# Rotated q and k computed by feature instead of by token in a two-block transformer kernel on one core

## The chip, the core and the metric

One core of a Trainium2 chip runs the whole program in one launch. The metric is device time in microseconds (us) of that launch. Four compute engines run their own instruction streams in order and meet on semaphores: TensorE (PE: matmuls and transposes, out to PSUM), VectorE (DVE), ScalarE (ACT) and GpSimd (POOL). SyncE (SP) issues the loads of the weights.

## The reference, cut to what matters

A block with two kinds of attention and a feed-forward part is followed by a second block of two layers over 256 tokens of 1024 features. The change is in the second block:

```python
def rope(x, pos):                       # MLA (64 of 192 features of a head), MoBA (64)
    cos, sin = jnp.cos(ang), jnp.sin(ang)
    x1, x2 = x[..., : d // 2], x[..., d // 2:]
    return jnp.concatenate([x1 * cos - x2 * sin, x1 * sin + x2 * cos], -1)

def retnet_rotate(x, pos):              # retention: 256 features, partners are neighbours
    x1, x2 = x[..., 0::2], x[..., 1::2]
    out = jnp.stack([x1 * cos - x2 * sin, x2 * cos + x1 * sin], -1)

# even layer: retention of 4 heads of 256 and MLA of 8 heads side by side, one output projection
q_r, k_r = retnet_rotate(_heads(rq, 4), pos), retnet_rotate(_heads(rk, 4), pos)
q_pe, k_pe = rope(q_m[..., 128:], pos), rope(mkr[:, None], pos)
# odd layer: MoBA of 16 heads of 64; with 256 tokens it is causal attention
q, k = rope(_heads(q, 16), pos), rope(_heads(k, 16), pos)
```

Every feature of a rotated head is its own value times a cosine plus its partner's value times a sine.

## The kernel before, in words

All weights come as 235 pieces of 128 x 1024 numbers. Each is split by ScalarE (`w_hi`, L1061) and VectorE (`w_lo`, L1205) into two parts, and TensorE forms every product as three matmuls (L792 to L794). A *chunk* is the set of pieces of one projection; a ring of six split pieces lies ahead of TensorE. A chunk of kind A (4 pieces, 512 output features) has the tokens as its output rows: 48 matmuls that stream 512 weight columns. A chunk of kind F (1 or 2 pieces, 128 features each) has the features as its output rows: 24 matmuls a piece that stream 256 tokens. Kind C is `mqkv`, the latents of MLA, by token.

`plan()` writes one list of steps, ORDER, and each engine runs its own part of it in that order. Jobs (a pair of attention heads: `scores`, `soft` on VectorE, `exp` on ScalarE, `norm` on VectorE, `pt` and `pv` on TensorE) wait in `pending` and are put, one step after each half piece, between the matmuls of later chunks, as soon as the names they need are in `given`. When a chunk's last matmul has been listed, its `evac` step follows at once.

Rotated chunks (`rk`, `rq` of retention, `mk`, `mq` of MoBA, 512 features each, and the 256 features of `mlaq`) are by token. VectorE multiplies with cosine (L1238) and sine (L1240, L1241), GpSimd adds and subtracts (L1538, L1539), and TensorE turns the result (`turn` steps on `rot`, L977), 2 x 2 transposes at a time; ScalarE copies them to `qT`, `kT` or `qpeT` (L1066). The turns are listed no earlier than four half pieces after the `evac` (`TURN_WAIT`), and only then is the chunk's name given. `kpe`, the rotated part of MLA's k, is 64 columns of `mqkv` with a turn of its own. The angle tables (L1375 to L1388 on VectorE, L1185 and L1186 on ScalarE) are made between the last up projection and the down projection of the first block; the split of the next pieces stands behind them on both engines.

Of the kernel before, what the change touches and what calls it, by code (L numbers as in the profile page):

```python
# [18 lines left out]
ALU = mybir.AluOpType  # L19
# [42 lines left out]
def chunks():  # L62
# [28 lines left out]
    for j in range(FT):  # L91
# [6 lines left out]
    add("mqkv", "C", 8, "X", k8, "dve", ("rms",),  # L98
        ("w_in_even", None, cols(MQ, 256) + cols(MKR, 32) + cols(MKV, 256) + cols(MKR + 32, 32)))

    def mla(half):
        for a in (0, 1):
# [5 lines left out]
             + [c for h in heads for c in cols(192 * h + 128, 64)]), after_job=16 + 4 * half)  # L108
# [4 lines left out]
    def ret_qk(pair):  # L113
        for name, c0 in (("k", RK), ("q", RQ)):
            add(f"r{name}{pair}", "A", 4, "X", k8, "dve", ("rope", name, 1 - pair, 256),
                ("w_in_even", None, [c0 + 256 * h + c for h in (2 * pair, 2 * pair + 1) for c in even_perm]),
                after_job=24 * pair)
# [9 lines left out]
    ret_qk(0)  # L127
    mla(1)
    for r in (0, 1):
        ret_vg(r)  # L130
    ret_qk(1)
# [5 lines left out]
    for half in (0, 1):  # L137
        s = 1 - half
# [3 lines left out]
        add(f"mv{half}", "A", 4, "X", k8, "act", ("copy_tok", s), ("w_in_odd", None, cols(2048 + 512 * half, 512)),  # L142
            after_ret=4)
        for a in (0, 1):
            add(f"mgt{half}{a}", "F", 2, "X", k8, "dve", ("gate", s, a),
                ("w_in_odd", None, cols(3072 + 512 * half + 256 * a, 256)), after_ret=4)
# [42 lines left out]
for h in range(8):  # L189
    JOBS.append(dict(kind="mla", s=0, h=h % 4, qk=[f"mlaq{h // 4}", f"mlakv{h // 4}"], v=f"mlakv{h // 4}",  # L190
                     g=f"mg{h // 4}{h // 2 % 2}", tile=h))
for h in range(16):
    JOBS.append(dict(kind="moba", s=1 - h // 8, h=h % 8, qk=[f"mk{h // 8}", f"mq{h // 8}"], v=f"mv{h // 8}",
                     g=f"mgt{h // 8}{h // 4 % 2}", tile=h // 2))
# [14 lines left out]
def plan():  # L209

    order, given, pending, deferred = [], set(), [], []
    state = dict(hi=0, lo=0, wait=0, credit=0)
# [31 lines left out]
    def flush_turns():  # L244

        while deferred:
            rope_turns()

    def evacuate(c):
        name, kind = CH[c]["name"], CH[c]["evac"][0]  # L250
        if kind in ("rope", "mla_q", "rms"):
            flush_turns()
        emit(("evac", c))
        if kind in ("rope", "mla_q"):
            deferred.append((name, 0))
            state["wait"] = TURN_WAIT
        else:
            given.add(name)

    def run(name, rate, needs=lambda i: set(), early=0, between=(), tail=()):  # L260
# [13 lines left out]
        for x, half in enumerate(halves):  # L274
# [24 lines left out]
            if deferred:  # L299
                state["wait"] -= 1  # L300
                if state["wait"] <= 0:
                    rope_turns()
# [8 lines left out]

    def rope_turns():

        name, i = deferred.pop()
        kind = CH[BY[name]]["evac"]
        dst = ("attn", kind[1], kind[2]) if kind[0] == "rope" else ("qpe",)
        emit(("turn", new_t(("rot", i), dst + (i,), False, 3, BY[name], 2)))
        if kind[0] == "rope" and i == 0:
            deferred.append((name, 2))
        else:  # L320
            given.add(name)
# [37 lines left out]
    def retention(r):  # L359
        s = set([f"rk{r // 2}", f"rq{r // 2}"])  # L360
# [57 lines left out]
    for name in ("mg00", "mg01"):  # L418
# [7 lines left out]
    for name in ("rk0", "rq0"):  # L426
        run(name, 1)
# [13 lines left out]
    for name in ("rk1", "rq1"):  # L441
        run(name, 1)
# [12 lines left out]
    rest = norm_second(2, CH[BY["mk0"]]["u0"] + 3)  # L455
# [47 lines left out]
for _s in ORDER:  # L503
    if _s[0] == "turn":
# [6 lines left out]
        else:  # L511
            _seen[d[:3] if d[0] == "attn" else d[:1]] = ("turn", _s[1])
# [3 lines left out]
    elif _s[0] in ("mm", "scores", "ret_s"):  # L516
        FILLED[_s] = dict(_seen)

ROT_READ, _r = {}, None
for _s in ORDER:  # L520
    if _s[0] == "turn" and TJ[_s[1]]["src"][0] in ("rot", "mn", "kpe"):
        _r = _s[1]
    elif _s[0] == "evac":
        ROT_READ[_s[1]] = _r
# [5 lines left out]
for _name, _n in (("ident", P), ("causal", 3 * P), ("band", P), ("cumA", 4), ("cumB", 4),  # L530
                  ("inv64", 32), ("inv256", 128)):
# [5 lines left out]
def constants():  # L537
# [17 lines left out]
    put("inv64", (1.0 / (np.float32(10000.0) ** (np.arange(0, 64, 2, dtype=np.float32) / np.float32(64)))).astype(np.float32)[None, :])  # L555
# [1082 lines left out]
```

## Time and profile before

| | us |
|---|---|
| median of 3 runs | 821.38 (820.64 to 822.02) |
| the profiled execution | 821.49 |
| its span, first to last instruction | 819.7 |
| TensorE busy | 767.2 (94%) |
| VectorE busy | 517.0 (63%) |
| ScalarE busy | 390.9 (48%) |
| GpSimd busy | 78.4 (10%) |

Times in the rows are counted from the span's start. The ends of matmuls are modelled, so the cost of one is read from start to start. A number in brackets at a row's end is the idle time of its engine before it, and what ended it. The granted clock is a share of TensorE's 2.4 GHz; 0.50 is 1.2 GHz.

### The profile page before, as it was taken

Reading aid. Unit: us, or ns where it says so; the run is one execution under the profiler, and the core shown is the slowest. Engines: PE = TensorE matmul, PEld = TensorE weight load, DVE = VectorE, ACT = ScalarE, POOL = GpSimd, SP = SyncE. Lnnn points to the kernel's source line nnn. Section 1 sums busy time; section 2 is a strip of 40 time slices with the busy share of each in tenths; the row PEclk is TensorE's granted clock in tenths of the full one; section 3 lists DMA queues with packets and bytes.
Section 4 is the critical chain, followed back from the end, with each engine's and each line's share of the span. In section 5 each row is a group of like instructions: output and inputs, shape, how many; then the busy total and the mean of one; then the engine's idle time right before and its main releaser. Section 6 shows DMA issues by size and latency. Waiting matters only on the chain.

```text
span 819.7 us, 12104 instructions
## 1 busy us (share of the span) xinstructions
PE 767.2 (94%) x4530; PEld 651.9 (80%) x4530; DVE 517.0 (63%) x910; ACT 390.9 (48%) x645; POOL 78.4 (10%) x98
## 2 busy tenths in 40 slices
PE   6999997999999999798988999999999989999995
PEld 5986875999999878697778777777788867777774
DVE  4554667677777764774565465855574497567575
ACT  5554662665656453264445544343434333563650
POOL 0000000011111100011031000220000014004000
PEclk9999999899999999999999999999999999999999
DMA  9742343455656574165326336344666616435402
GB/s 332 282 154 79 112 138 138 154 190 171 203 165 197 170 279 141 55 217 181 105 93 196 110 103 205 123 143 147 205 225 190 200 52 210 151 114 168 156 27 78
DMA packets 37291, 130.28 MB, mean 159 GB/s; under 512 B 4401, under 2 KB 4657, under 8 KB 37105
## 3 DMA queue, kind: packets, MB, share of 16 engines
q1 hardware_dynamic: 36000, 125.04, 46.0%
q0 software_dynamic: 1232, 4.46, 1.7%
q8 instruction: 37, 0.61, 0.3%
q14 instruction: 22, 0.17, 0.1%
HBM read 128.43 MB, written 1.05 MB: 158 GB/s over the span
## 4 chain that ended last, share of the span: by engine, by line
PE 83%; DVE 9%; POOL 3%; ACT 2%; issue 2%; DMA 1%; DVEq 0%; SPq 0%; ACTq 0%
PE acc L792 25%; PE acc L794 23%; PE acc L793 23%; PE acc L903 2%; PE acc L977 2%; PE acc L922 1%; POOL rot L1538 1%; PE acc L942 1%; POOL rot L1539 1%; DVE small L1401 1%; DVE res L1425 1%; DVE res L1393 1%; PE acc L901 1%; DVE res L1435 1%; DMA res<-in_x 1%
## 5 line engine op out<-in xcount | busy, mean ns | idle before, releaser
L1205 DVE TENSOR_TENSOR w_lo<-raw,w_hi 128x1024 fp32r<-128x1024 f32 (+2 forms) x235 | 282.6, 1228 | 89.5 <-ACT w_hi L1061 89.4
L1061 ACT ACTIVATE w_hi<-raw 128x1024 fp32r<-128x1024 f32 (+2 forms) x235 | 237.5, 1036 | 73.6 <-PE acc L794 66.3
L792 PE MATMUL acc<-X_hi,w_hi 128*128 128x256 f32 x616 | 179.0, 291 | 3.9 <-DVE w_lo L1205 2.9
L793 PE MATMUL acc<-X_lo,w_hi 128*128 128x256 f32 x616 | 176.3, 286 | 0.0
L794 PE MATMUL acc<-X_hi,w_lo 128*128 128x256 f32 x616 | 176.1, 286 | 0.0
L792 PE MATMUL acc<-w_hi,X_hi 128*128 128x512 f32 (+1 forms) x352 | 141.7, 402 | 9.3 <-DVE X_lo L1212 4.5
L794 PE MATMUL acc<-w_hi,X_lo 128*128 128x512 f32 (+1 forms) x352 | 135.4, 385 | 0.0
L793 PE MATMUL acc<-w_lo,X_hi 128*128 128x512 f32 (+1 forms) x352 | 135.2, 384 | 0.0
L792 PEld LDWEIGHTS acc<-X_hi,w_hi 128*128 128x128 f32 x616 | 120.2, 195 | 8.5 <-issue 4.0
L793 PEld LDWEIGHTS acc<-X_lo,w_hi 128*128 128x128 f32 x616 | 120.4, 195 | 0.1
L794 PEld LDWEIGHTS acc<-X_hi,w_lo 128*128 128x128 f32 x616 | 120.2, 195 | 0.0
L792 PE MATMUL acc<-w_hi,S_hi 128*128 128x512 f32 (+1 forms) x264 | 104.2, 395 | 2.4 <-DVE w_lo L1205 2.4
L793 PE MATMUL acc<-w_lo,S_hi 128*128 128x512 f32 (+1 forms) x264 | 102.1, 387 | 0.0
L794 PE MATMUL acc<-w_hi,S_lo 128*128 128x512 f32 (+1 forms) x264 | 102.0, 386 | 0.0
L792 PEld LDWEIGHTS acc<-w_hi,X_hi 128*128 128x128 f32 x352 | 66.8, 190 | 26.6 <-issue 10.1
L794 PEld LDWEIGHTS acc<-w_hi,X_lo 128*128 128x128 f32 x352 | 66.8, 190 | 13.1
L793 PEld LDWEIGHTS acc<-w_lo,X_hi 128*128 128x128 f32 x352 | 67.0, 190 | 11.4 <-issue 0.7
L792 PEld LDWEIGHTS acc<-w_hi,S_hi 128*128 128x128 f32 x264 | 49.6, 188 | 14.3 <-DVE w_lo L1205 2.8
L1306 DVE SCALAR_TENSOR_TENSOR v<-acc,cvp,v 128x255 f32<-128x255 f32 (+1 forms) x88 | 38.4, 478 | 32.6 <-ACT v L1126 31.8
L794 PEld LDWEIGHTS acc<-w_hi,S_lo 128*128 128x128 f32 x264 | 49.6, 188 | 10.3
L793 PEld LDWEIGHTS acc<-w_lo,S_hi 128*128 128x128 f32 x264 | 49.7, 188 | 9.5 <-issue 0.2
L1126 ACT ACTIVATE v<-acc,cvp 128x256 f32<-128x256 f32 x44 | 22.5, 562 | 50.4 <-PE acc L794 50.4
(147 smaller groups left out, 729.2 us busy)
## 6 DMA issues: line engine op xcount, KB each, us to landing
raw<-in_w SPq DMA_DIRECT2D x225, 512.0 KB, 4.2
raw<-in_w SPq DMA_DIRECT2D x8, 288.0 KB, 2.8
gate<-in_ln_gain POOLq DMA_DIRECT2D x4, 512.0 KB, 4.3
gate<-in_ln_bias POOLq DMA_DIRECT2D x4, 512.0 KB, 4.9
res<-in_x SPq DMA_DIRECT2D x4, 256.0 KB, 3.6
gate<-in_bias SPq DMA_DIRECT2D x1, 1024.0 KB, 10.3
out<-res SPq DMA_DIRECT2D x4, 256.0 KB, 2.1
decay<-in_decay SPq DMA_DIRECT2D x1, 512.0 KB, 10.3
```

Source lines behind the costliest of these rows:

```text
L792: nc.tensor.matmul(out, a_hi, b_hi, start=start, stop=False)
L793: nc.tensor.matmul(out, a_hi, b_lo, start=False, stop=False)
L794: return nc.tensor.matmul(out, a_lo, b_hi, start=False, stop=stop)
L901: nc.tensor.matmul(dst, qT[s][:, h, q], kT[s][:, h, 0:nk], start=True, stop=False)
L903: last[i] = nc.tensor.matmul(dst, qT[s][rows, h // 2, q], kT[s][rows, h // 2, 0:nk], start=True, stop=kind != "fox")
L922: last = nc.tensor.transpose(job[:, 2, b * P:(b + 1) * P], pr[:, j % 2, b * P:(b + 1) * P], ident)
L942: last = nc.tensor.matmul(job[i * HD:(i + 1) * HD, 3, q0:q0 + n], vv[s][:, tt, v], ptb[:, (j + i) % 2, b0:b0 + n], start=tt == 0, stop=tt ...
L977: last = nc.tensor.transpose(out[:, i * S + tt * P:i * S + (tt + 1) * P], src[:, i * P:(i + 1) * P], ident)
L1061: nc.scalar.activation(w_hi[:, u % RING, 0:n], raw[:, u % RAW, 0:n], ACT.Copy).then_inc(hi_done, 1)
L1126: last = nc.scalar.activation(conv[j % 2][:, i, :], acc[:, b0, i * S:(i + 1) * S], ACT.Identity, scale=cvp[:, 2, i, j:j + 1], bias=cvp[:, ...
L1205: nc.vector.tensor_tensor(w_lo[:, u % RING, 0:n], raw[:, u % RAW, 0:n], w_hi[:, u % RING, 0:n].bitcast(F32), ALU.subtract).then_inc(lo_don ...
L1306: last = nc.vector.scalar_tensor_tensor(o, acc[:, b0, i * S:i * S + S - lag], cvp[:, 2 - lag, i, j:j + 1], o, ALU.mult, ALU.add)
```

## The change

Rotated chunks become kind F: their features are the output rows, as `qT` and `kT` want them, and nothing rotated is transposed. A retention head is a chunk of its own (`rk0` to `rk3`, `rq0` to `rq3`); MoBA's `mk` and `mq` are four chunks of 256 features each; the rotated columns of `mlaq` are by feature too, and `kpe` is a chunk of one piece, its 64 columns twice. `mqkv` keeps 2 x 256 columns a token instead of 2 x 288.

Of a head of 256, the partners lie in the two 128-row tiles. Of a head of 64, weight columns are permuted (`turn_perm`) so that partners are 16 rows apart in a group of 32; VectorE's shuffle exchanges them. The tables have one row a feature and one column a token (128 x 256, for 64 and for 256), from positions that are loaded to all 128 partitions. GpSimd multiplies by the sine, then adds, each over 128 x 512 (for 256: as before, two of 128 x 256). Attention waits for `rope_done`, which GpSimd's last step sets. A name is given with its `evac` step. In MoBA the order of the chunks is new, and all 16 heads are listed as one sequence.

```diff
+    turn_perm = [32 * e + 16 * g + i for g in (0, 1) for e in (0, 1) for i in range(16)]
-        ("w_in_even", None, cols(MQ, 256) + cols(MKR, 32) + cols(MKV, 256) + cols(MKR + 32, 32)))
+    add("mqkv", "C", 8, "X", k8, "dve", ("rms",), ("w_in_even", None, cols(MQ, 256) + cols(MKV, 256)))
+    add("kpe", "F", 1, "X", k8, "dve", ("rope", "kpe", 0, 0, 64), ("w_in_even", None, [MKR + i for i in turn_perm] * 2))
...
-            add(f"r{name}{pair}", "A", 4, "X", k8, "dve", ("rope", name, 1 - pair, 256),
+            add(f"r{name}{r}", "F", 2, "X", k8, "dve", ("rope", name, 1 - r // 2, 2 * (r % 2), 256),
...
-            add(f"m{name}{half}", "A", 4, "X", k8, "dve", ("rope", name, s, 64), ("w_in_odd", None, cols(c0 + 512 * half, 512)),
-                after_ret=4, by_token=(name, half) == ("k", 0))
+            add(f"m{name}{half}{a}", "F", 2, "X", k8, "dve", ("rope", name, 1 - half, 2 * a, 64),
+                ("w_in_odd", None, [c0 + 512 * half + 256 * a + 64 * h + i for h in range(4) for i in turn_perm]), after_ret=4)
...
     def evacuate(c):
-        name, kind = CH[c]["name"], CH[c]["evac"][0]
-        if kind in ("rope", "mla_q", "rms"):
-            flush_turns()
         emit(("evac", c))
-        if kind in ("rope", "mla_q"):
-            deferred.append((name, 0))
-            state["wait"] = TURN_WAIT
-        else:
-            given.add(name)
+        given.add(CH[c]["name"])
...
-    emit(("turn", new_t(("kpe", 0), ("kpe", 0), False, 3, 0)))
     for i in (0, 2):
-        emit(("turn", new_t(("mn", i), ("S", 20 + i), True, 3, 0, 2)))
+        emit(("turn", new_t(("mn", i), ("S", 20 + i), True, i // 2, 0, 2)))
...
-    run("mk0", 0, early=3, between=rest)
-    run("mq0", 0)
-    attention(range(24, 32))
-    for name in ("mv0", "mgt00", "mgt01", "mk1", "mq1"):
-        run(name, 1)
-    attention(range(32, 40))
-    for name in ("mv1", "mgt10", "mgt11"):
+    run("mv0", 0, early=3, between=rest)
+    for name in ("mk00", "mq00", "mgt00"):
+        run(name, 0)
+    attention(range(24, 40))
+    for name in ("mk01", "mq01", "mgt01", "mk10", "mq10", "mv1", "mgt10", "mk11", "mq11", "mgt11"):
         run(name, 1)
...
-        ang = qT[0][:, 0:2, 0:160]
+        ang = qT[0][:, 0:2, :]
...
+                    if BY[name] in ROPES:
+                        pe.wait_ge(rope_done, ROPES.index(BY[name]) + 1)
...
+                cos = tab[:, 0, int(wide), :].unsqueeze(1).to_broadcast([P, nt, S])
+                if wide:
+                    sin = tab[:, 1, 1, :]
+                    nc.vector.tensor_tensor(part[:, 0, :], x[:, 1, :], sin, ALU.mult)
+                    nc.vector.tensor_tensor(part[:, 1, :], x[:, 0, :], sin, ALU.mult)
+                else:
+                    nc.vector.stream_shuffle(part, x, [i ^ 16 for i in range(32)])
+                nc.vector.tensor_tensor(out, x, cos, ALU.mult).then_inc(evac_dve, 1)
...
+                if rope_width(c) == 256:
+                    nc.gpsimd.tensor_tensor(out[:, 0, :], out[:, 0, :], part[:, 0, :], ALU.subtract)
+                    nc.gpsimd.tensor_tensor(out[:, 1, :], out[:, 1, :], part[:, 1, :], ALU.add).then_inc(rope_done, 1)
+                else:
+                    nc.gpsimd.tensor_tensor(part, part, sin, ALU.mult).then_inc(pool_chain, 1)
+                    pool.wait_ge(pool_chain, chained[0])
+                    nc.gpsimd.tensor_tensor(out, out, part, ALU.add).then_inc(rope_done, 1)
```

Three places show how the steps move. The first is TensorE where the first scores of MoBA's second half of heads stand (`pr` transposes are L905 and L922, scores L886 and L903). Before, behind the first half of the third piece of `mv1`, with the second turn of `mq1` between:

```order
L793 MATMUL acc<-w_lo,X_hi 128x512
L794 MATMUL acc<-w_hi,X_lo 128x512
L977 MATMUL acc<-cst,rot 128x128 [waits rot_ready,t_hi]
L977 MATMUL acc<-cst,rot 128x128
L977 MATMUL acc<-cst,rot 128x128 [waits rot_ready]
L977 MATMUL acc<-cst,rot 128x128
L903 MATMUL acc<-kT,qT 128x128 [waits t_hi,max_done]
```

Now, behind the last matmuls of `mq10`:

```order
L774 MATMUL acc<-X_lo,w_hi 128x256
L775 MATMUL acc<-X_hi,w_lo 128x256
L905 MATMUL acc<-cst,pr 128x128 [waits pt_copied,p_done]
L905 MATMUL acc<-cst,pr 128x128 x2
L886 MATMUL acc<-kT,qT 128x128 [waits rope_done,max_done]
```

Between the last matmul of the rotated q and the scores that read it, five half pieces of `mv1` and two turns have become three transposes of `pr`; the scores wait for GpSimd itself. The scores of heads 12 to 15 stand behind `mq11` in the same way, those of heads 4 to 7 one half piece behind `mq01`, and those of heads 0 to 3 five half pieces behind `mq00`.

The second place is VectorE for the same chunk (L1205 and L1194 are splits of weights, L1333 and L1313 the softmax of the scores above). Before:

```order
L1238 TENSOR_TENSOR rot<-acc,tab 128x512 [waits t_ready,rot_ready,ry_done,w_used]
L1240 TENSOR_TENSOR rtmp<-acc,tab 128x8x32
L1241 TENSOR_TENSOR rtmp<-acc,tab 128x8x32
L1238 TENSOR_TENSOR rot<-acc,tab 128x512
L1240 TENSOR_TENSOR rtmp<-acc,tab 128x8x32
L1241 TENSOR_TENSOR rtmp<-acc,tab 128x8x32
L1205 TENSOR_TENSOR w_lo<-raw,w_hi 128x1024 [waits w_used,hi_done] x2
L1333 ISA pr,small<-acc,cst 128x128 [waits pt_ready,sc_ready]
```

Now:

```order
L1194 TENSOR_TENSOR w_lo<-raw,w_hi 128x1024 [waits w_used,hi_done] x2
L1223 STREAM_SHUFFLE rtmp<-acc 128x512 [waits rope_done,ry_done,w_used]
L1224 TENSOR_TENSOR qT<-acc,tab 128x512
L1313 ISA pr,small<-acc,cst 128x128 [waits pt_ready,sc_ready]
L1313 ISA small 128x1
```

Six instructions for 512 features are two for 256, and the softmax follows with no split between. The third place is VectorE behind `mq01` (L1321 to L1323 are the `norm` of head 3, for which the `pt` after the next half piece waits). Now:

```order
L1194 TENSOR_TENSOR w_lo<-raw,w_hi 128x1024 [waits w_used,hi_done]
L1223 STREAM_SHUFFLE rtmp<-acc 128x512 [waits rope_done,ry_done,w_used]
L1224 TENSOR_TENSOR qT<-acc,tab 128x512
L1321 RECIPROCAL small<-small 128x2 [waits exp_done]
L1322 TENSOR_SCALAR pr<-pr,small 128x128 [waits dve_chain]
L1323 TENSOR_SCALAR pr<-pr,small 128x256
```

A rotation stands ahead of a `norm` there; it does so behind `mk01`, `rk0` and `rq0` too. Before, no rotation of MoBA stood ahead of a `norm`.

## Rows read from the trace of the kernel before

**Rows 1.** the page's part 4, the chain that ended last: shares by engine
```profile
PE 83%; DVE 9%; POOL 3%; ACT 2%; issue 2%; DMA 1%; DVEq 0%; SPq 0%; ACTq 0%
```

**Rows 2.** TensorE by stretch: length, busy (instructions), granted clock, DMA
```profile
153.00:273.00 120.00, 120.00 (x1002) 1.00 0.56 184
606.68:640.68 34.00, 34.00 (x151) 1.00 0.67 218
352.60:358.20 5.60, 5.60 (x45) 1.00 0.98 328
```

**Rows 3.** TensorE's timeline: start, duration, work, [idle before <- its releaser]
```profile
684.07 0.38 PE L977 MATMUL acc<-cst,rot 128*128 128x128 f32 x2
...
685.28 0.48 PE L792 MATMUL acc<-w_hi,X_hi 128*128 128x512 f32 x1
...
686.76 0.60 PE L977 MATMUL acc<-cst,rot 128*128 128x128 f32 x4
687.11 0.48 PE L792 MATMUL acc<-w_hi,X_hi 128*128 128x512 f32 x1
```

**Rows 4.** TensorE's waits in 359:660, then in 676:800: us in total, times, longest
```profile
PE acc L792 <- ACT kT L1088: 3.2, 2, 1.6
PE acc L922 <- DVE pr L1343: 2.1, 1, 2.1
...
PE acc L977 <- POOL rot L1539: 1.3, 2, 0.6
...
PE acc L977 <- POOL rot L1539: 1.9, 3, 0.6
PE acc L922 <- DVE pr L1343: 1.7, 4, 0.4
PE acc L903 <- ACT qT L1066: 1.6, 2, 0.8
```

**Rows 5.** timeline of TensorE around the transposes of the latents
```profile
371.58 0.38 PE L977 MATMUL acc<-cst,ryb 128*128 128x128 f32 x2
...
375.18 0.36 PE L792 MATMUL acc<-S_hi,w_hi 128*128 128x256 f32 x1
```

**Rows 6.** the largest wait, and two stretches with their granted clock
```profile
142.85 1.09 PE L961 MATMUL acc<-cst,res 128*128 128x128 f32 x4 [4.69 <-DVE res L1435]
...
143.00:150.35 7.35, 6.93 (x31) 0.50 0.17 50
375.60:379.05 3.45, 3.45 (x19) 0.51 0.00 0
```

**Rows 7.** timelines of TensorE, VectorE and GpSimd around rotations
```profile
691.31 0.39 PE L792 MATMUL acc<-w_hi,X_hi 128*128 128x512 f32 x1
...
691.51 0.69 DVE L1238 TENSOR_TENSOR rot<-acc,tab 128x512 f32<-128x512 f32 x1 [1.31 <-PE acc L794]
...
410.65 0.81 DVE L1343 TENSOR_SCALAR pr<-pr,small 128x256 f32<-128x256 f32 x1
...
382.16 0.47 POOL L1538 TENSOR_TENSOR rot<-rot,rtmp 128x128 f32<-128x128 f32 x1 [18.86 <-DVE rtmp L1241]
...
692.94 0.74 POOL L1538 TENSOR_TENSOR rot<-rot,rtmp 128x256 f32<-128x256 f32 x1 [7.91 <-DVE rtmp L1241]
...
694.34 1.72 POOL L1538 TENSOR_TENSOR rot<-rot,rtmp 128x256 f32<-128x256 f32 x1
```

**Rows 8.** timelines of VectorE, ScalarE, TensorE around the angle tables
```profile
279.52 0.27 DVE L1375 CAST small<-posi 128x2 f32<-128x2 int32 x1
...
281.15 1.54 DVE L1383 SCALAR_TENSOR_TENSOR qT<-qT 128x320 f32<-128x320 f32 x3
...
284.57 0.26 ACT L1185 ACTIVATE tab<-kT 128x64 f32<-128x64 f32 x1 [4.13 <-DVE kT L1388]
...
287.84 0.50 PE L792 MATMUL acc<-w_hi,S_hi 128*128 128x512 f32 x1 [2.39 <-DVE w_lo L1205]
```

**Rows 9.** timeline of ScalarE: the copy of v of the first MLA half
```profile
388.72 1.03 ACT L1091 ACTIVATE v<-acc 128x1024 f32<-128x1024 f32 x1
```

More of the change, by code:

```diff
@@ L107, in mla @@
             ("w_uq_even", [0, 1], [c for h in heads for c in cols(192 * h, 128)]
-             + [c for h in heads for c in cols(192 * h + 128, 64)]), after_job=16 + 4 * half)
+             + [192 * h + 128 + i for h in heads for i in turn_perm]), after_job=16 + 4 * half)
         add(f"mlakv{half}", "Q2", 2, "S", [22, 23], "act", ("mla_kv", half),
@@ L127, in chunks @@
     ret_qk(0)
+    ret_qk(1)
     mla(1)
@@ L310, in run @@
                 state["credit"] -= 1
[L312 to L321, printed above, removed]
     def attention(jobs):
@@ L425, in plan @@
     attention(range(16, 20))
-    for name in ("rk0", "rq0"):
+    for name in ("rk0", "rq0", "rk1", "rq1"):
         run(name, 1)
@@ L440, in plan @@
         run(name, 1)
-    for name in ("rk1", "rq1"):
+    for name in ("rk2", "rq2", "rk3", "rq3"):
         run(name, 1)
@@ L511 @@
         else:
-            _seen[d[:3] if d[0] == "attn" else d[:1]] = ("turn", _s[1])
+            raise ValueError(d)
     elif _s[0] == "ylo":
@@ L515 @@
             _seen[("S", JOBS[_j]["tile"])] = ("y", _s[1] // 2)
-    elif _s[0] in ("mm", "scores", "ret_s"):
+    elif _s[0] == "mm":
         FILLED[_s] = dict(_seen)
[L519 to L524, printed above, removed]
+MN_TURN = [_s[1] for _s in ORDER if _s[0] == "turn" and TJ[_s[1]]["src"][0] == "mn"]
 RET_TURN = {r: max((n for n in RANK if TJ[n]["src"][:2] == ("ry", r)), key=RANK.get) for r in range(4)}
@@ L618, in build @@
         rgain = pr[:, :, :].rearrange("p b n -> p (b n)")[:, 0:512]
[L619 to L624 removed]
+        ang = qT[0][:, 0:2, :]
+        turns = qT[0][:, 2:4, :]
+        wrap = qT[1][:, 0:2, :]
+        sin_arg = kT[0][:, 0:2, :]
+        cos_arg = kT[0][:, 2:4, :]
+        posi = ptb[:, 0, 0:S].bitcast(I32)
+        posf = ptb[:, 1, 0:S]
+        latent = rot
         bforget = small[:, 80:81]
@@ L870, in mm @@
                                          hi[:, k, :], lo[:, k, :], x == 0, x == 1)
+                elif kind == "Q1":
+                    for x, k in enumerate(tiles):
+                        w = slice(x * 256 + part * P, x * 256 + part * P + P)
+                        last = three(acc[:, b0 + 2, part * S:(part + 1) * S], wh[:, w], wl[:, w], hi[:, k, :], lo[:, k, :],
+                                     x == 0, x == 1)
                 else:
-                    n = 256 if kind == "Q1" else 512
                     for x, k in enumerate(tiles):
-                        w = slice(x * n, x * n + n)
-                        last = three(acc[:, b0 + 2 + part, 0:n], hi[:, k, part * P:(part + 1) * P],
+                        w = slice(x * 512, x * 512 + 512)
+                        last = three(acc[:, b0 + 2 + part, :], hi[:, k, part * P:(part + 1) * P],
                                      lo[:, k, part * P:(part + 1) * P], wh[:, w], wl[:, w], x == 0, x == 1)
@@ L889, in scores @@
                 bank_free(pe, step)
-                seen = FILLED[step]
-                if kind in ("mla", "moba"):
-                    keys = [("qpe",), ("kpe",)] if kind == "mla" else [("attn", "q", s), ("attn", "k", s)]
-                    pe.wait_ge(t_hi, max(RANK[seen[k][1]] for k in keys) + 1)
                 for tt, c0, nk in ((0, 0, P), (1, P, S)):
@@ L1032, in y_dest, with rope_dest, rope_width, rope_part @@
             return S_hi[:, tile, :], S_lo[:, tile, :], yb[:, j // 2 % 2 * S:(j // 2 % 2 + 1) * S]
+        def rope_dest(c):
+            e = CH[c]["evac"]
+            if e[0] == "mla_q":
+                return qpeT[:, :, :]
+            if e[1] == "kpe":
+                return kpeT[:, :, :]
+            return (qT if e[1] == "q" else kT)[e[2]][:, e[3]:e[3] + 2, :]
+        def rope_width(c):
+            return 64 if CH[c]["evac"][0] == "mla_q" else CH[c]["evac"][4]
+        def rope_part(c):
+            nt = rope_dest(c).shape[1]
+            return rtmp[:, ROPES.index(c) % 2, 0:nt * S].rearrange("p (k s) -> p k s", k=nt)
         def t_dest(n):
@@ L1215, in rope @@
                 ch = CH[c]
-                kind = ch["evac"][0]
-                heads, d = (512 // ch["evac"][3], ch["evac"][3]) if kind == "rope" else (1, 64) if kind == "rms" else (4, 64)
-                b0, half, r = ch["bank"], d // 2, ROT.index(c)
-                tab = tab64 if d == 64 else tab256
+                r, out, part = ROPES.index(c), rope_dest(c), rope_part(c)
+                nt = out.shape[1]
+                bank = ch["bank"] + (2 if ch["evac"][0] == "mla_q" else 0)
+                x = acc[:, bank, 0:nt * S].rearrange("p (k s) -> p k s", k=nt)
```

192 lines of the change are left out of this document (70 added, 122 removed).

## The prediction, made before the changed kernel ran

> **What bounds the kernel now.** I read the chain that ended last first: TensorE holds 83% of it [rows 1]. So time changes by what TensorE has to do and by what it waits for, and nothing else. The second view gives its price of work, from start to start. In a stretch of F chunks 1,000 matmuls of 256 columns (two more hang over the edges) take 120 us: 0.120 each. In a stretch of 512-column matmuls 150 take 34.0 us: 0.2267 each. In `mqkv` 42 of 288 columns take 5.60 us: 0.133 each [rows 2]. The third view is the turns. One that waits for nothing takes 0.35 (686.76 to 687.11), one that waits 0.64 for GpSimd takes 1.21 (684.07 to 685.28), so such a wait costs 0.2 more than its own length; and the first matmul behind a turn lasts 0.48 where others last 0.39, 0.1 more [rows 3]. The fourth is TensorE's waits: in both layers of the second block they belong mostly to this change's parts [rows 4]. The fifth is the clock: behind a wait of 4.69 it was half for 7.35 us of TensorE's work, and it was half once more right behind the turns of the latents; waits of 2.1 and 2.39 left it up [rows 4, 6, 8].
>
> **What goes.** 18 turns of rotated tiles (8 chunks of two, `mlaq` two) at 0.35 and about 0.1 behind each: 8.0. Their waits: for GpSimd 1.3 + 1.9, for the copy of q 1.6 and once more in retention, which I take as 0.8, and 3.2 where the copy of `kT` stood on ScalarE behind the copy of a turn [rows 4]: 8.8, and 0.2 more for each of ten: 2.0. From the turn of `kpe` to the first `mlaq` matmul 3.60 go by [rows 5]. The two turns of the latents now use two banks and need not wait for each other; what is left is one turn, ScalarE's copy and VectorE's difference, two operations of 128x512 at 0.7 [rows 7] and 0.3 to drain, with hops 2.2: 1.4 saved. With less idle time there the stretch at half clock, 3.45 us long, should go: half of it, 1.6 [rows 6]. Sum: **-21.8**.
>
> **What TensorE must do more.** Eight A chunks of 48 x 0.2267 = 10.88 become 96 x 0.120 = 11.52: +5.1. `mqkv` falls by 96 x 0.0133 = 1.3, `kpe` adds 24 x 0.120 = 2.9: +1.6. Sum: **+6.7**.
>
> **The angle tables.** VectorE works from 279.52 to 284.5 on them, ScalarE ends them, and only then comes the split for which TensorE waits 2.39 [rows 8]. They grow from 320 to 512 numbers a row. At nothing but a fixed cost they would add 0, in full proportion 0.6 x 5.0 = 3.0. One such operation over 320 takes 0.51 (281.15), one over 512 about 0.69 (691.51) [rows 7, 8], 35 to 40% more: +2.0 with ScalarE's part. This path has no cover, so the wait becomes 4.4. That lies near the 4.69 that cost the clock. Half clock costs half its length, between 0 and 3.7 (7.35 / 2) [rows 6], 1.7 for a stretch like the one at 375; with the chance that it comes I take 1.5. Sum: **+3.5**.
>
> **The rotation as a wait.** VectorE starts 0.20 after TensorE's next start (691.31, 691.51), and 128x512 from PSUM takes it 0.69 [rows 7]. The shuffle has no row. Its bounds are half of that and double; I take the same 0.69, since it streams as many numbers. The Trainium skill, "VectorE: DVE Perf Modes", section on the perf-mode tier table, gives about 2400 ns for a shuffle of 2048 numbers with no faster mode; an estimate from that page is 0.6 for 512. GpSimd takes 0.47 for 128x128 and 0.74 for 128x256 [rows 7], 0.27 per 128, so 1.28 for 512; bounds are 0.74 and the 1.72 of an operation that was held up. GpSimd's two depend on each other. The Trainium skill, "GPSIMD Engine Reference", section "Elementwise — side-by-side cycle accounting", has 2.6 cycles a number for two inputs; an estimate is 1.1 for 512 without the start, and that page speaks against arithmetic on this engine. Chain: 0.20 + 2 x 0.69 + 0.1 + 1.28 + 0.1 + 1.28 = 4.35 us from the chunk's end to the scores.
>
> What covers it decides. In retention 10 us of other chunks do, and before MoBA's first scores five half pieces (7.2 us); no wait there, even if each GpSimd operation is held 1 us by a split. Before the scores of heads 8 and of 12 there is only one `pt` (three transposes, like a turn 0.35): 4.0 each, **+8.0**. TensorE's whole queue stands behind them; VectorE's next is the softmax of the same scores. Each such wait may cost the clock, 1.4 each by chance: **+2.8**. Behind `mv1` follows its first `pv` directly: 0.2 + 1.03 for the copy [rows 9] + 0.1: **+1.3**.
>
> Then the `norm` behind a rotation. At 410.65 an operation of VectorE over 128x256 took 0.81 beside GpSimd's rotation, more than the 0.69 of one twice as wide [rows 7]; so behind a rotation `norm` first waits for one GpSimd operation. `mk01`: 0.20 + 1.38 + 0.1 + 1.28 + 0.3 = 3.3 against `pt` and a half piece, 1.8: **+1.5**. `mq01`: the scores of heads 4 to 7 need both GpSimd operations and, between them, the `norm`: 4.5 against 2.2 (`pt`, half piece, `pt`): **+2.3**. `rk0` and `rq0` have 128x256 operations: 1.3 each, for which the 2.1 there now goes: about 0. Of the four waits of 0.43 for `pr` two go: **-0.9**.
>
> **Sum:** -21.8 + 6.7 + 3.5 + 8.0 + 2.8 + 1.3 + 1.5 + 2.3 - 0.9 = +3.4. The profiled execution took 821.49, so 824.9; it stands 0.1 above the median. I say **825**. The 18 copies that ScalarE loses and the load of positions on SyncE's queue I cost at nothing: ScalarE runs ahead of TensorE there, and the load has five raw pieces ahead of it; without that cover it would be a microsecond or two once.
>
> **Rivals.** *The clock stays up.* The three long waits come, but none halves it, as 2.39 did not: 825 - 4.3 = 820.7. For it: only one wait of this length is in the trace, and at 4.69 it is longer than all of mine. Against: at 375 less sufficed. 0.20.
>
> *Faster: GpSimd's operation hardly grows.* If 128x512 costs the 0.74 of 128x256, the chain is 2.2 of GpSimd's time less 1.1, that is 1.1 shorter: 3.3 at three scores, 0.5 at `mk01`, and the two long waits of 2.9 then leave the clock up, 2.8: 825 - 6.6 = 818.4. It decides below some 0.85 an operation. Against it: 0.47 to 0.74. 0.13.
>
> *Slower still: GpSimd holds back the splits.* An operation of GpSimd beside a split of two SBUF inputs took 1.72 for 0.74: they take turns [rows 7]. Now one of GpSimd's lasts 1.28 and there are 16 in MoBA. Where four of them end in a late `w_lo`, that is 4 x 1.28 = 5.1: 830. It decides where VectorE falls behind its lead of four pieces; the place is `mk01` and `mq01`, where each chunk's splits, rotation, two softmaxes and two norms stand beside 2.6 us of GpSimd. For it speaks that every rotation in the trace was held up so, against it that TensorE waited for no `w_lo` behind one. The Trainium skill, "SBUF — State Buffer", section "Who interferes with whom", calls this port pair an exclusive lock that the loser waits out; the trace agrees with 1.72 for 0.74. 0.22.
>
> **Numbers.** My forecast holds 0.45: 822 to 828. A measurement tells about 0.2%, 1.6 us, from no change: faster is below 819.8, slower above 823.0. Forecast: 0.40 slower, 0.05 same. Clock stays up: 0.05 faster, 0.13 same, 0.02 slower. Small GpSimd cost: 0.13 faster. Port: 0.22 slower. Faster 0.18, same 0.18, slower 0.64. Of the bounds, a shuffle of half or double time moves three scores by 1.0 to 2.1, the tables move it by -2.0 to +1.0. Leaving a tenth at each end: 818.5 to 830.5.
>
> **What would show it.** No matmul on `rot`; F matmuls at 0.120; the wait at the first down pieces 4.4 instead of 2.39, the shuffle at 0.7; a wait of 4 for GpSimd before two `scores`, of 1 before one more, and 1.3 before one `pv`; the clock at half behind some of them; no waits for `kT` of 1.6. It is wrong if the waits before the scores are under 3 us, if the removed waits come back elsewhere in the even layer (the `pt` behind `rk0`, the first MLA scores behind `mlakv`), or if `w_lo` ends waits in MoBA.

## The result and the profile after

| | before | after |
|---|---|---|
| median | 821.15 us (820.64 to 822.02, 4 runs) | 827.65 us (4 runs; the three that count: 825.02, 826.69, 828.62) |
| ratio after / before | | 1.0072, 95% interval 1.0049 to 1.0096 |
| the profiled execution | 821.49 | 828.62 |
| its span | 819.7 | 826.8 |
| TensorE's mean granted clock | 0.987 | 0.978 |

The change makes the kernel 0.7% slower. The fourth run of after took 1087 us at a mean clock of 0.654; it is in the median and not in the ratio, and differences from the changed kernel are taken below from 826.69, the middle one of the three that count. The profiled execution is the slowest of those three: what is read from it adds up to 7.1 us, where the medians (826.69 and 821.15) lie 5.5 apart. The kernel before, measured beside every experiment, took 821.04 to 821.54. The page of the changed kernel, first the busy times, then the shares of the chain that ended last, answers to [rows 1]:

```profile
PE 768.2 (93%) x4864; PEld 670.5 (81%) x4864; DVE 524.3 (63%) x901; ACT 382.1 (46%) x625; POOL 89.8 (11%) x88
...
PE 84%; DVE 9%; issue 2%; ACT 2%; DMA 1%; POOL 1%; SPq 0%; DVEq 0%; ACTq 0%
```

TensorE is busy 1.0 us longer than before and the span is 7.1 longer: what was added is waiting. (A matmul at half clock counts as busy for longer, so some of the 1.0 is clock as well.) The totals of TensorE's waits, the even layer first (359:660), then MoBA (670:805), answer to [rows 4]:

```profile
PE acc L905 <- DVE pr L1323: 2.7, 2, 1.3
PE acc L773 <- DVE gate L1240: 1.5, 1, 1.5
...
PE acc L886 <- POOL qT L1509: 9.7, 3, 4.9
PE acc L905 <- DVE pr L1323: 3.1, 3, 1.3
PE acc L925 <- ACT v L1076: 1.1, 1, 1.1
```

In the even layer (retention and MLA) the waits for `kT`, for `rot` and for `qT` are gone. In MoBA three `scores` (L886) wait for GpSimd for 9.7 us in all. Next I cut both executions at five places where TensorE starts the same piece of work; each number is the difference of two start times, and the five sum to the spans:

| TensorE from ... to ... | before | after | difference | by the terms of the prediction |
|---|---|---|---|---|
| start to the first up projection | 145.45 | 146.58 | +1.1 | none: nothing there is touched |
| to the down matmul behind the tables | 142.39 | 144.41 | +2.0 | +2.0 |
| to the first matmul of `mqkv` | 52.03 | 53.58 | +1.6 | +1.5 |
| to the first matmul of MoBA | 324.10 | 313.53 | -10.6 | -9.5 |
| to the end of MoBA's layer and of the program | 155.73 | 168.70 | +13.0 | +9.5 |

The first row is a start that differs from execution to execution: over all profiles of this study the `turn` ahead of it begins anywhere from 141.9 to 144.0. The last column splits the terms by layer: the even one loses ten turns (4.4), waits (5.3 and 1.0), 1.4 at the latents and 1.6 of clock, and gains 1.6 and 2.6 of work; MoBA loses eight turns (3.6), waits (3.5 and 1.0) and 0.9, and gains 2.6 of work and 8.0 + 2.8 + 1.3 + 1.5 + 2.3.

**The tables.** ScalarE, VectorE and TensorE, as [rows 8] before:

```profile
287.40 0.63 ACT L1173 ACTIVATE tab<-kT 128x512 f32<-128x512 f32 x1 [5.71 <-DVE kT L1367]
...
288.64 4.83 ACT L1051 ACTIVATE w_hi<-raw 128x1024 fp32r<-128x1024 f32 x5
289.71 5.76 DVE L1194 TENSOR_TENSOR w_lo<-raw,w_hi 128x1024 fp32r<-128x1024 f32 x5 [2.35 <-ACT w_hi L1051]
290.99 0.50 PE L773 MATMUL acc<-w_hi,S_hi 128*128 128x512 f32 x1 [4.29 <-DVE w_lo L1194]
```

The wait is 4.29 where 2.39 was. All three engines take part in it: VectorE computes the angles, ScalarE takes the sines and then splits, and VectorE idles 2.35 for that split.

**The scores of head 8.** VectorE, GpSimd and TensorE behind `mq10`; its last matmul ends just before 734.32:

```profile
733.23 2.36 DVE L1194 TENSOR_TENSOR w_lo<-raw,w_hi 128x1024 fp32r<-128x1024 f32 x2 [1.43 <-ACT w_hi L1051]
734.32 0.49 PE L905 MATMUL acc<-cst,pr 128*128 128x128 f32 x3
...
735.52 0.73 DVE L1223 STREAM_SHUFFLE rtmp<-acc 128x512 f32<-128x512 f32 x1
736.14 0.67 DVE L1224 TENSOR_TENSOR qT<-acc,tab 128x512 f32<-128x512 f32 x1
736.89 1.26 POOL L1507 TENSOR_TENSOR rtmp<-rtmp,tab 128x512 f32<-128x512 f32 x1 [4.27 <-DVE qT L1224]
738.23 1.26 POOL L1509 TENSOR_TENSOR qT<-qT,rtmp 128x512 f32<-128x512 f32 x1
739.75 1.65 PE L886 MATMUL acc<-kT,qT 64*128 64x128 f32 x8 [4.94 <-POOL qT L1509]
```

The chain of the prediction stands there link by link: shuffle, multiply, two GpSimd operations of 1.26. From the shuffle's start it takes 4.23. The shuffle itself starts 1.2 after the chunk's end, 1.0 later than it could: two splits stand ahead of it. Behind `mq11` nothing does; there TensorE waits 3.95, and from the chunk's end (776.93) to the scores (781.37) 4.44 go by, for which I had 4.35.

**The norm behind a rotation.** VectorE, GpSimd and TensorE behind `mk01`:

```profile
697.67 0.67 DVE L1224 TENSOR_TENSOR kT<-acc,tab 128x512 f32<-128x512 f32 x1
...
698.42 1.26 POOL L1507 TENSOR_TENSOR rtmp<-rtmp,tab 128x512 f32<-128x512 f32 x1 [8.11 <-DVE kT L1224]
698.45 1.32 DVE L1322 TENSOR_SCALAR pr<-pr,small 128x128 f32<-128x128 f32 x1
699.69 0.34 DVE L1323 TENSOR_SCALAR pr<-pr,small 128x256 f32<-128x256 f32 x1
...
700.09 0.55 PE L905 MATMUL acc<-cst,pr 128*128 128x128 f32 x3 [1.35 <-DVE pr L1323]
```

The same L1322 takes 0.28 where GpSimd rests (715.72); here it takes 1.32 and ends with GpSimd's operation.

**The clock.** TensorE by stretch, with the granted clock behind the counts:

```profile
291.68:295.09 3.41, 3.41 (x10) 0.50 0.93 299
...
711.52:714.93 3.41, 3.41 (x17) 0.50 0.02 5
738.82:745.65 6.83, 5.90 (x18) 0.50 0.12 43
779.78:786.61 6.83, 5.24 (x25) 0.50 0.25 79
```

These four are at half clock; the kernel before had none behind its tables and none in MoBA. It had two in the even layer, the one at 375.60 [rows 6] and one at 348.33, the first of the rows here. In this execution they are gone; the second row is the changed kernel from behind the tables into MoBA, at full clock throughout:

```profile
348.33:351.74 3.41, 3.41 (x16) 0.50 0.50 150
...
296.00:700.00 404.00, 387.28 (x2226) 1.00 0.50 164
```

Half of TensorE's time in a stretch at half clock is the loss. In MoBA these are 3.41 / 2 + 5.90 / 2 + 5.24 / 2 = 7.3, in the even layer -3.4.

The second 1.7 of that -3.4 is not the change's doing. The stretch at 348.33 begins among the short waits at the start of `mqkv`, which stand in every kernel here, and nine of the twelve profiled executions are at half clock there (this row is from the changed kernel with its tables moved, see below):

```profile
344.77:348.18 3.41, 3.31 (x15) 0.50 0.36 96
```

The three that are not are the changed kernel, the kernel before with its tables moved, and `norm_first`. That the clock stayed up there in the changed kernel's profile is chance, as far as these runs show.

### The profile page after: what moved, and what is told of

The parts are those of the page before. It is cut to its first block, busy times and chain, and to the rows that moved or that the text cites. A ratio compares the mean times of both kernels' runs of the same rounds, so it can differ in the third digit from the quotient of the medians.

```text
span 826.8 us, 12730 instructions
## 1 busy us (share of the span) xinstructions
PE 768.2 (93%) x4864; PEld 670.5 (81%) x4864; DVE 524.3 (63%) x901; ACT 382.1 (46%) x625; POOL 89.8 (11%) x88
## 4 chain that ended last, share of the span: by engine, by line
PE 84%; DVE 9%; issue 2%; ACT 2%; DMA 1%; POOL 1%; SPq 0%; DVEq 0%; ACTq 0%
PE acc L773 25%; PE acc L775 24%; PE acc L774 24%; PE acc L886 2%; PE acc L925 1%; DVE small L1380 1%; DVE res L1404 1%; PE acc L905 1%; DVE res L1372 1%; PE acc L884 1%; DMA res<-in_x 1%; DMA raw<-in_w 1%; DVE res L1414 1%; ACT w_hi L1051 1%; DVE X_lo L1201 1%
## 5 line engine op out<-in xcount | busy, mean ns | idle before, releaser
L1194 DVE TENSOR_TENSOR w_lo<-raw,w_hi 128x1024 fp32r<-128x1024 f32 (+1 forms) x236 | 285.4, 1236 | 91.1 <-ACT w_hi L1051 91.0
L1051 ACT ACTIVATE w_hi<-raw 128x1024 fp32r<-128x1024 f32 (+1 forms) x236 | 237.7, 1034 | 87.2 <-PE acc L775 80.8
L773 PE MATMUL acc<-X_hi,w_hi 128*128 128x256 f32 x880 | 256.4, 291 | 3.9 <-DVE w_lo L1194 2.9
L774 PE MATMUL acc<-X_lo,w_hi 128*128 128x256 f32 x880 | 252.2, 287 | 0.0
L775 PE MATMUL acc<-X_hi,w_lo 128*128 128x256 f32 x880 | 251.9, 286 | 0.0
L773 PEld LDWEIGHTS acc<-X_hi,w_hi 128*128 128x128 f32 x880 | 172.2, 196 | 10.6 <-issue 6.0
L773 PE MATMUL acc<-w_hi,S_hi 128*128 128x512 f32 x256 | 102.5, 400 | 4.3 <-DVE w_lo L1194 4.3
L775 PE MATMUL acc<-w_hi,S_lo 128*128 128x512 f32 x256 | 100.4, 392 | 0.0
L774 PE MATMUL acc<-w_lo,S_hi 128*128 128x512 f32 x256 | 100.3, 392 | 0.0
L773 PE MATMUL acc<-w_hi,X_hi 128*128 128x512 f32 (+1 forms) x224 | 88.8, 396 | 6.2 <-DVE X_lo L1201 4.5
```

Source lines behind the costliest of these rows:

```text
L773: nc.tensor.matmul(out, a_hi, b_hi, start=start, stop=False)
L774: nc.tensor.matmul(out, a_hi, b_lo, start=False, stop=False)
L775: return nc.tensor.matmul(out, a_lo, b_hi, start=False, stop=stop)
L1051: nc.scalar.activation(w_hi[:, u % RING, 0:n], raw[:, u % RAW, 0:n], ACT.Copy).then_inc(hi_done, 1)
L1194: nc.vector.tensor_tensor(w_lo[:, u % RING, 0:n], raw[:, u % RAW, 0:n], w_hi[:, u % RING, 0:n].bitcast(F32), ALU.subtract).then_inc(lo_don ...
```

## The experiments

My theory after the result was that the change itself saves time, and that it is slower because of where its results are waited for: two `scores` right behind their rotated q, a `norm` behind the rotation, tables without cover. Cover is TensorE's other work between the end of a chunk and the step that reads its result. The rivals were: the lock between VectorE and GpSimd is the cause, GpSimd is the wrong engine, or the F chunks cost more than the turns they replace. The first kernels alter one thing each; the last ones put them together. An experiment's ratio is to the kernel before, measured beside it.

**Scores one half piece later.** A rotated MoBA chunk's name is held back for n half pieces of later chunks (the number in `held` is counted down after each half piece, and at zero the name is given); here n is 1.

```diff
         emit(("evac", c))
-        given.add(CH[c]["name"])
+        if CH[c]["name"][:2] in ("mk", "mq"):
+            held.append([CH[c]["name"], n + 1])
+        else:
+            given.add(CH[c]["name"])
...
```

> The names of rotated MoBA chunks are given one half piece (1.4 us) later, so the scores of heads 8 and of 12 get 1.4 us of cover; nothing else changes. Theory (the scores wait for a chain that is a fixed time behind the chunk's end): 4.94 becomes 3.5 and 3.95 becomes 2.5, 2.9 us less. If both waits still cost the clock (some 3 us each in the changed kernel: 6.8 us at half clock, of which 0.9 lies in the wait), 824.7. If one of 2.5 leaves it up, as 2.39 did in the kernel before, 821.8. Rival (the wait is VectorE and GpSimd being behind with splits, so it moves along with whatever stands there): both waits stay within 0.5 of what they were, 827.6.

Measured: 823.84 (820.47 to 826.27, 12 runs). The waits were 3.55 and 2.53, 1.39 and 1.42 shorter for 1.4 of cover. The rival is out: the chain is a fixed time. Both long waits still cost the clock in the profiled execution (825.59), so 2.53 doesn't leave it up there; the two short waits at `mq01` (1.34 and 0.78) do. The fastest of the 12 runs lies 5.8 below the slowest. The mean granted clocks go with the times: the five runs from 820.47 to 821.85 have 0.982 to 0.984, the five from 825.50 to 826.27 have 0.974 to 0.979 (one of 824.46 has 0.982). So the clock makes most of that spread, but only the run of 825.59 has a trace.

**Scores three half pieces later**, n is 3.

> The names of rotated MoBA chunks are given three half pieces (4.3 us) later. Theory: waits of 0.78, 4.94 and 3.95 before scores become 0, 0.6 and 0, and the pv behind mv1 (1.1) gets a half piece of cover: 10 us less; the two stretches at half clock behind the scores go, 5.9 more: 811.5, and 809.8 if the third stretch (behind the transposes after mq01) goes too. Rival (lock): behind the later scores a split now stands beside both GpSimd operations, which then take 2.2 each instead of 1.3, the chain is 6.2 and waits of 1.7 stay at each of the two: 815. Rival (the loss is not in the waits but in TensorE's own work, F chunks and transposes): under 3 us gained, 825 or more.

Measured: 814.96, ratio 0.9928 [0.9911, 0.9946]: 11.7 gained, and that is the end of the rival that TensorE's own work is the loss. My theory's 811.5 was too low by 3.5; the number is that of the lock's rival (815), though its waits were 1.7 and 1.7 and the measured ones 2.95 at head 8 and 0.61 at head 12. GpSimd and VectorE there:

```profile
732.64 0.67 DVE L1231 TENSOR_TENSOR qT<-acc,tab 128x512 f32<-128x512 f32 x1
733.24 1.21 DVE L1201 TENSOR_TENSOR w_lo<-raw,w_hi 128x1024 fp32r<-128x1024 f32 x1
733.39 2.17 POOL L1514 TENSOR_TENSOR rtmp<-rtmp,tab 128x512 f32<-128x512 f32 x1 [6.05 <-DVE qT L1231]
...
735.65 1.26 POOL L1516 TENSOR_TENSOR qT<-qT,rtmp 128x512 f32<-128x512 f32 x1
737.16 1.23 PE L893 MATMUL acc<-kT,qT 64*128 64x128 f32 x6 [2.95 <-POOL qT L1516]
```

The operation of 1.26 takes 2.17 beside the split. So the lock (one of the two engines held while the other works) is real and costs 0.9 an operation, but at these scores only once there is something else to do: in the changed kernel VectorE had nothing to split while TensorE stood still. The stretch behind this wait was at half clock again (6.83 us); that behind head 12 was not, nor that behind `mq01`. One more was at half clock than in the changed kernel, at 350.79 in the even layer, which this edit leaves alone.

**All of the rotation on VectorE.** Both GpSimd operations are issued by VectorE, in place of L1507 and L1509 (and L1502, L1503).

```diff
                 nc.vector.tensor_tensor(out, x, cos, ALU.mult).then_inc(evac_dve, 1)
...
+                    link(nc.vector.tensor_tensor(part, part, sin, ALU.mult))
+                    nc.vector.tensor_tensor(out, out, part, ALU.add).then_inc(rope_done, 1)
```

> Both GpSimd operations of every rotation are done by VectorE instead. Theory: a 128x512 operation takes VectorE about 0.69 against 1.28, the chain behind a chunk is 0.2 + 4 x 0.69 + 0.2 = 3.2 instead of 4.35: the waits before the scores of heads 8 and 12 fall to 3.8 and 2.8; with the clock still lost 825.3, with one of the two stretches saved 822.3. The norm behind mk01, rk0 and rq0 no longer waits for GpSimd, but for two more operations of its own engine: no change there. Rival (VectorE has no room; its splits come late in MoBA): w_lo ends waits of TensorE and the time is above 829. Rival (GpSimd's lock on splits and norms is the main loss): splits beside rotations fall from 2.3 to 1.2, and the time is below 820.

Measured: 822.17, 4.5 less than after, and what I had expected with one of the two stretches saved (822.3): that of head 12 was at half clock for 3.28 us of work instead of 5.24. The waits before the scores of heads 8 and 12 are 4.12 and 2.72 (4.94 and 3.95), the one behind `mq01` (0.78) is gone. The `pt` behind `mk01` and `mq01` wait 1.77 (1.35), where I had expected no change. An operation of VectorE takes 0.69 against 1.26. No `w_lo` ended a wait behind a rotation, and the time is not below 820 either: both rivals fail, the chain's length is what counts.

**Later and on VectorE.**

> As the run with the scores three half pieces later (814.96), and VectorE does GpSimd's two operations of every rotation. There the scores of head 8 still waited 2.95 and lost the clock, because splits beside GpSimd's operation made it 2.17 instead of 1.3. Theory (that lock is what is left): from the shuffle's start (1.0 late, behind a split) four operations at 0.67 take 2.7, the wait falls to 0.9, that of head 12 from 0.6 to 0, the first pt behind mk01 waits 0.4 more (1.77, as in the run with all on VectorE); 2.3 less, and 3 more if the clock stays up: 809.7 (812.7 if it falls). Rival (VectorE's added work makes splits late): w_lo ends waits of TensorE, 815 or more.

Measured: 809.22, ratio 0.9849 [0.9836, 0.9863], for 809.7. No scores wait (I had 0.9 at head 8), and no stretch of MoBA is at half clock.

**The norm ahead of the rotation**, in the changed kernel.

```diff
             if x == len(halves) - 1:
+                if name[:2] in ("rk", "rq", "mk", "mq") and pending and "norm" in [st[0] for st in pending[0][1]]:
+                    background()
+                    state["credit"] -= 1
                 evacuate(c)
```

> The changed kernel with one thing altered: behind mk01, mq01, rk0 and rq0 the norm is listed ahead of the rotation; scores and tables stay where they are. Theory (a norm that stands behind the rotation is held by its two operations and by GpSimd's first, 1.3 us each time): the waits of the pt behind mk01 (1.35), rk0 and rq0 (1.33 each) go; behind mq01 the rotation itself now starts 0.8 later, and what the pt gains (1.34) the scores of head 4 lose: their wait grows from 0.78 to about 2.9. Together 4.0 less and 0.8 more: 824.4. Rival (waits of 1.3 cost the clock as well, and it comes back): 822 or less. Rival (the exponentials are late, not the norms): 827.

Measured: 819.06, 7.6 less, where I had 3.2 less. The four `pt` waits went (5.35 in all), and the scores of head 4 wait 2.36 instead of 0.78, as expected in kind. What I had not seen is that the two splits ahead of the shuffle at `mq10` now begin 3.8 before the chunk's end instead of 1.1, so the shuffle starts on time (0.2 behind it, 728.26) and the scores wait 3.95 for 4.94. A `pt` that waited also cost some 0.2 beside its wait, and a wait of 0.66 at a `pv` (415.47 in the changed kernel) goes too. The rival that waits of 1.3 cost the clock has the better number, but no stretch in the even layer was at half clock before this edit, so its reason isn't there. About 1.2 of the profiled difference (820.75 against 828.62) lies ahead of the first up projection.

**The rotation ahead of the split**, in the changed kernel.

```diff
+            elif x == len(halves) - 1 and name[:2] in ("mk", "mq"):
+                evacuate(c)
+                split_to(u + AHEAD + 1)
             else:
                 split_to(u + AHEAD + 1)
...
```

> The changed kernel with one thing altered: the rotation of a MoBA chunk is listed ahead of the split that stood before it on VectorE. Behind mq10 the shuffle waited 1.0 for that split. Theory (VectorE and GpSimd take turns; a split beside GpSimd's operation makes it 2.2 instead of 1.3): the 1.0 is gained at mq10 and lost again in GpSimd's operations, and at mq11, where nothing was late, 0.9 is lost: waits of 4.9 and 4.9 before the scores instead of 4.94 and 3.95, 827 to 829. Rival (no lock that matters): 3.95 and 3.95, 826.6.

Measured: 830.85, 4.2 more, above the 827 to 829 that I had expected. At `mq11`, where nothing had been late:

```profile
779.80 0.67 DVE L1228 TENSOR_TENSOR qT<-acc,tab 128x512 f32<-128x512 f32 x1
780.39 1.21 DVE L1198 TENSOR_TENSOR w_lo<-raw,w_hi 128x1024 fp32r<-128x1024 f32 x1
780.55 2.17 POOL L1511 TENSOR_TENSOR rtmp<-rtmp,tab 128x512 f32<-128x512 f32 x1 [1.30 <-DVE qT L1228]
782.80 1.26 POOL L1513 TENSOR_TENSOR qT<-qT,rtmp 128x512 f32<-128x512 f32 x1
...
784.32 1.06 PE L890 MATMUL acc<-kT,qT 64*128 64x128 f32 x6 [4.86 <-POOL qT L1513]
```

The wait grew by 0.9, just what the split adds to GpSimd's operation. At `mq10` it is 5.64, 0.7 more: the shuffle was still 0.8 late behind an earlier split (1.0 in the changed kernel), and the 0.9 came on top. The `pt` behind `mk01` and `mq01` wait 2.25, since the norm now stands behind the split too. This is the plainest sign of the lock. In this profile the clock was also at half at 351.05 and 658.25, where it was up in the changed kernel, so not all of the 4.2 is the lock. (Where a split and GpSimd's second operation overlap too, as behind `mk11`, both of GpSimd's operations take over 2.1.) The Trainium skill, "SBUF — State Buffer", section "Who interferes with whom", says that a VectorE operation with two inputs in SBUF contends with GpSimd's reads, and one with at most one such input, outside the two-port modes, doesn't; the trace agrees: the split holds GpSimd (2.17 for 1.26), and a multiply out of PSUM with one table from SBUF neither is held nor holds. In the kernel before it takes 0.68 beside the GpSimd operation that starts at 692.94 [rows 7] and takes its usual 0.74, and 0.69 with none beside it:

```profile
692.78 0.68 DVE L1238 TENSOR_TENSOR rot<-acc,tab 128x512 f32<-128x512 f32 x1
```

No trace has the shuffle beside GpSimd for more than 0.15 us. L1322 of the `norm` has one input in SBUF and is held all the same; no row tells in which mode it ran.

**The tables inside the down projection**, made after its eighth half piece, in the changed kernel and in the kernel before.

```diff
+            if (name, x) == ("down", 8):
+                emit(("tables",))
...
-    emit(("tables",))
     emit(("load", "ln", 1))
```

> The angle tables are made after the eighth half piece of the down projection instead of before its first. Theory (their whole cost is the wait of 4.29 at the first down pieces and the stretch at half clock behind it, 3.4 us long): 4.3 + 1.7 less, 821.7. Rival (VectorE is behind at the end of the up projections anyway and the wait for its split stays at 2 or more, clock up): 823.6. Rival (the 7 us in a row only move the wait into the down projection): 827.

Measured: 820.47 (817.69 to 821.74), ratio 0.9989 [0.9973, 1.0005], 6.2 less than after, for 6.0 expected. The wait is gone and so is the stretch at half clock behind it; no other wait grew. A stretch at half clock is new at the start of `mqkv` (344.77, the row above). The stretches behind the scores of heads 8 and 12 were at half clock for 3.41 each (in the changed kernel 5.90 and 5.24), though the waits ahead of them were the same 4.95 and 3.95.

> The kernel before, by token, with its angle tables (320 numbers a row) inside the down projection instead of ahead of it. Theory: its wait of 2.39 at the first down pieces is all that they cost, since the clock stayed up there: 2.5 less than before, 818.9. Rival (there is a clock loss behind it that the profiled execution did not show): 817 or less. Rival (the wait only moves into the down projection): no change.

Measured: 815.95, ratio 0.9936 [0.9922, 0.9949]: 5.6 less than the 821.54 of the kernel before beside it, which is the first rival's number. The wait (2.39) is gone. The profile of this kernel has neither of the stretches at half clock that the one of before had at 348.33 and 375.60, though the waits ahead of them are the same, but a new one, behind the `pt` that waits 2.11 for a norm, which left the clock up before:

```profile
405.57:408.98 3.41, 3.41 (x10) 2.63 (x9) 2.09 (x3) 2.90 (x4) 0.16 (x1) 0.50 0.00 0
```

So a wait of about 2 costs 1.7 more in one execution and nothing in another, and an edit that moves all that follows by a few microseconds can change which stretches are at half clock. Against a kernel before with its tables covered, the change has to beat 815.95, not 821.

**All together.** Later scores, tables in down, norm first: once on VectorE with n = 3, once with GpSimd and n = 4.

> As the run before in this call, with the angle tables made inside the down projection, and with the norm listed ahead of the rotation where the two stood in the other order (behind mk01, mq01, rk0, rq0). Theory: the parts add up: 4.3 and 1.7 of clock for the tables, 1.7 + 1.15 + 1.15 for the three pt that waited, so 10 less than that run: 799.7, and both kernels are beaten by 20. Rival (the parts share their losses, and a gain in one is given back in the next): the sum comes to half, 805.

Measured: 796.58, ratio 0.9702 [0.9685, 0.9719]: 3.1 below what I had expected from the parts, and far from the rival's 805.

> The rotation stays on GpSimd; scores four half pieces later, tables inside the down projection, norm ahead of the rotation. Theory (a chain that is only made longer by the lock needs cover, not another engine): from 814.96, tables 6.0, norms 4.0, the waits before the scores 2.95 to 1.5 and 0.6 to 0, clock 3 if it stays up at 1.5: 800.3. Rival (the engine matters more than the cover; splits beside GpSimd's operations now come late too): more than 4 us above the run with VectorE in this call.

Measured: 796.26, ratio 0.9693 [0.9680, 0.9706], 4.0 below what I had expected, with a wait of 0.3 where I had 1.5; the rival is out. TensorE's waits in MoBA and the end of the even layer, then the page's chain, of this last kernel:

```profile
PE acc L784 <- DVE X_lo L1212: 2.3, 2, 1.4
PE acc L955 <- DVE res L1425: 0.5, 1, 0.5
PE acc L784 <- DVE w_lo L1205: 0.4, 1, 0.4
PE acc L897 <- POOL qT L1520: 0.3, 1, 0.3
...
PE 88%; DVE 7%; DMA 1%; issue 1%; ACT 1%; POOL 1%; SPq 0%; DVEq 0%; ACTq 0%
```

Of all waits for a rotation 0.3 us is left, though both GpSimd operations behind `mq10` take 2.2 there. With enough cover the engine doesn't matter. This version beats both kernels: 25.3 us under the kernel before, 30.4 under the changed one, and 19.7 under the kernel before with its tables moved. That last kernel still has a `pt` that waits 2.11 for a `norm` behind a rotation; listing that `norm` first might take the wait off there too, which no run tests. Nor does any run separate the new order of MoBA's chunks from the rest of the change.

## Why the prediction was right, and where its sizes were off

Forecast 825.0 (range 818.5 to 830.5), slower with 0.64; measured 827.65 (826.69 over the three runs that count), slower. The waits and their order are right by mechanism. That the total came this close is in part luck: the clock cost more in MoBA than I had, and a stretch at half clock in the even layer was absent in the profiled execution for no reason in the change.

- **What goes and TensorE's added work.** Net -9.5 for the even layer by my terms, -10.6 measured. The second stretch at half clock (348.33), which I hadn't counted, is worth 1.7 of that, so without it the layer gives 8.9. The stretch that I did count (375.60) is in none of the kernels by feature, but the kernel before with its tables moved doesn't have it either, with its turns in place: that the 1.6 comes from the shorter waits is not shown. The turns of the latents take 2.37 to the first `mlaq` matmul (376.49 to 378.86) for my 2.2. The new F matmuls run at 0.120 (18 in 2.16 us, from 774.77 to 776.93). Without its new waits the edit was to save 21.8 - 6.7 = 15.1; between the two kernels with covered tables, 815.95 and 796.26, lie 19.7, in which the new order of the norms and the clock have a part.
- **The angle tables.** 4.4 predicted, 4.29 measured; 1.5 of clock, 1.7 measured. Moving the tables gave 6.2 for the 6.0 of the two.
- **The scores of heads 8 and 12.** 4.0 each; 4.94 and 3.95 measured. The chain was right to 0.1 (4.44 for 4.35); what I missed is the order ahead of it on VectorE, two splits, 1.0.
- **The shuffle and GpSimd's operation.** I took 0.69 and 1.28; they are 0.73 and 1.26. The rival in which GpSimd's operation hardly grows is refuted.
- **The norm behind a rotation.** `mk01` +1.5 (1.35), `mq01` +2.3 (1.34 + 0.78), `rk0` and `rq0` 1.3 each (1.33 and 1.33): right, and for the reason given. The `pv` behind `mv1`: 1.3, measured 1.1.
- **The clock: the term that was mis-sized.** "Each such wait may cost the clock, 1.4 each by chance: +2.8". Both did, for 2.95 and 2.62, and a third stretch came behind the two short waits at `mq01` (1.34 and 0.78, with a chain of transposes between), 1.7: 7.3 in all. I had priced a stretch by the shorter one of [rows 6], and only behind single long waits. The 7.3 is one execution's: with waits of 4.95 and 3.95 in the same places, the changed kernel with its tables moved lost 5.1 there (three stretches of 3.4).
- **The rival of the lock** had 0.22 and 830. It did not happen as put, since `w_lo` ended no wait behind a rotation in MoBA (one of 0.41, at 661.51, stands in the kernel before too, at 667.38); it happened at the norms, where I had it in the sum. Its price beside splits (0.9 an operation, not 1.28) showed in the edited kernels.
- **The end.** 1.1 of the 7.1 between the profiled executions lies in the start, ahead of the change.

The terms of MoBA sum to +9.5 for +13.0 measured: clock +4.5, the late shuffle +0.9, some shorter waits -1.0 (`mk01`, `mq01`, the `pv`, one more wait of 0.43 that went); -0.9 is not accounted for. That is the size by which the forecast fell short.

## What to carry to other kernels

A result that moves to another engine must be costed together with what is queued behind it and who reads it next: here the rotation by feature costs 5.5 us in one order and saves 19.7 in another (against a kernel before with its tables moved too). Before judging such a change, give each new result as many pieces of cover as its chain is long (here 4.4 us, or 6.3 where both GpSimd operations stand beside splits: 716.09 to 722.38 in the last kernel). Moving the chain to the faster engine took 0.8 and 1.2 off the two long waits; one half piece of cover took 1.4 off each. Short work with no cover, such as a table made once, belongs in a stretch where TensorE's lead is long.

## What the runs showed of the hardware

- Waits for less than I had thought cost the clock: 2.53 did (`late1`), 2.11 did once (tables in the down projection of the kernel before) and did not in the kernel before itself; 1.34 and 0.78 with three transposes between them did in the changed kernel and did not in `late1`. Behind 4.94 and 3.95 TensorE was at half clock for 5.90 and 5.24 us of its work in the changed kernel, and behind 4.95 and 3.95 for 3.41 each once the tables had moved.
- Runs of one kernel (`late1`) spread over 5.8 us, with the mean granted clock at 0.982 to 0.984 in the fastest five and 0.974 to 0.979 in the slowest five.
- A VectorE operation of 0.28 over 128x128 out of SBUF (L1322) takes 1.32 when GpSimd has begun 0.03 earlier. An operation of GpSimd of 1.26 takes 2.17 when a split has begun 0.15 earlier. In both cases the one that began first was not held.
- The shuffle of 128x512 out of PSUM takes 0.73, a multiply of the same size 0.67.
